# Moving the statistics tile, so that the working buffers begin at a whole kilobyte

## The reference

```python
# first block
proj = rmsnorm(x) @ w_in                       # q_r k_r v_r g_r | q_s k_s v_s | gate_r gate_s
ret = silu(g_r) * retention_chunkwise(q_r, k_r, v_r)      # 4 heads, chunks of 128
swa = swa_gqa_sinks(q_s, k_s, v_s, sinks)                 # 8 heads, window of 128
merged = sigmoid(gate_r) * (ret @ w_ret_out) + sigmoid(gate_s) * (swa @ w_swa_out)
x = x + rmsnorm(merged @ w_out)
x = x + rmsnorm(square(relu(rmsnorm(x) @ w_up)) @ w_down)
# second block
h = x @ w_in_2                                 # pooled part u | q k v | f_logit
mix = concat(pool_mixer(u), forgetting_attention(q, k, v, f_logit)) @ w_out_2
x = layer_norm(ALPHA * x + mix)
x = layer_norm(ALPHA * x + square(relu(x @ w_mlp1_2)) @ w_mlp2_2)
```

## Time and profile before

| | us |
|---|---|
| median of 3 runs | 2570.82 (2569.25 to 2571.11) |
| span of the profiled execution, first to last instruction | 2565.4 |
| TensorE busy | 2522.4 (98%) |
| VectorE busy | 1474.4 (57%) |
| ScalarE busy | 1057.2 (41%) |
| GpSimd busy | 189.9 (7%) |
| transfers, share of 16 engines' span | 38.6% |

### The profile page before, as it was taken

One profiled execution on the slowest core, in us unless ns is written; L12 is line 12 of the kernel. 1 busy time (PEld: TensorE's weight loads), 2 busy tenths in 40 slices (PEclk: granted clock), 3 DMA queues, 4 the chain that ended last, 5 costly groups with the idle time before them and its releaser, 6 DMA issues.

```text
span 2565.4 us, 30682 instructions
## 1 busy us (share of the span) xinstructions
PE 2522.4 (98%) x12072; PEld 2080.6 (81%) x12072; DVE 1474.4 (57%) x2153; ACT 1057.2 (41%) x1698; POOL 189.9 (7%) x173
## 2 busy tenths in 40 slices
PE   7999999999999999999999999999999999999998
PEld 6777888888887788888888887876788888888887
DVE  4345223323533877766764754358768676576668
ACT  4344322223212544444434542357526444444343
POOL 0000000000020200000000110145111000000000
PEclk9999999999999999999999999999999999999999
DMA  4211211111422426547865542101313364488554
GB/s 165 72 69 66 75 41 42 34 33 66 148 83 82 140 89 216 180 156 256 305 256 187 181 158 65 34 20 40 114 51 131 140 223 139 171 324 324 180 193 172
DMA packets 129679, 347.59 MB, mean 135 GB/s; under 512 B 13152, under 2 KB 13408, under 8 KB 129408
## 3 DMA queue, kind: packets, MB, share of 16 engines
q1 hardware_dynamic: 129536, 345.63, 38.6%
HBM read 256.91 MB, written 85.52 MB: 133 GB/s over the span
## 4 chain that ended last, share of the span: by engine, by line
PE 91%; DVE 4%; issue 2%; ACT 1%; DMA 1%; POOL 1%; SPq 0%; DVEq 0%; ACTq 0%; POOLq 0%
PE bank L643 28%; PE bank L645 28%; PE bank L644 28%; DVE PAl L2407 1%; DVE st L2402 1%; PE bank L704 1%; POOL accX L2588 1%; PE bank L754 1%; PE bank L821 1%; PE bank L1070 1%; PE bank L831 0%; PE bank L825 0%; PE bank L789 0%; ACT PAh L1680 0%; DVE wlo L1740 0%
## 5 line engine op out<-in xcount | busy, mean ns | idle before, releaser
L1740 DVE TENSOR_TENSOR wlo<-raw,whi 128x1024 fp32r<-128x1024 f32 x102 | 125.2, 1235 | 253.9 <-ACT whi L1143 253.2
L643 PE MATMUL bank<-hhi,whi 128*128 128x512 f32 x608 | 249.3, 410 | 1.6 <-DVE hlo L1765 1.6
L645 PE MATMUL bank<-hhi,wlo 128*128 128x512 f32 x608 | 238.9, 393 | 0.0
L644 PE MATMUL bank<-hlo,whi 128*128 128x512 f32 x608 | 238.2, 392 | 0.0
L1143 ACT ACTIVATE whi<-raw 128x1024 fp32r<-128x1024 f32 x102 | 106.6, 1054 | 103.8 <-PE bank L645 88.2
L643 PEld LDWEIGHTS bank<-hhi,whi 128*128 128x128 f32 x608 | 114.9, 189 | 29.1 <-issue 6.7
L645 PEld LDWEIGHTS bank<-hhi,wlo 128*128 128x128 f32 x608 | 114.7, 189 | 25.4
L644 PEld LDWEIGHTS bank<-hlo,whi 128*128 128x128 f32 x608 | 115.1, 189 | 22.5
L1448 ACT ACTIVATE r<-r 128x512 f32<-128x512 f32 x78 | 49.1, 629 | 137.6 <-DVE r L2225 100.0
L643 PE MATMUL bank<-yhi,whi 128*128 128x512 f32 x192 | 74.9, 390 | 0.0
L645 PE MATMUL bank<-yhi,wlo 128*128 128x512 f32 x192 | 74.7, 389 | 0.0
(11 more groups left out here) (477 smaller groups left out, 7197.0 us busy)
## 6 DMA issues: line engine op xcount, KB each, us to landing
ra<-ud_d SPq DMA_DIRECT2D x112, 512.0 KB, 4.5
raw<-wp_d SPq DMA_DIRECT2D x102, 512.0 KB, 3.5
rbh<-wp_d SPq DMA_DIRECT2D x64, 512.0 KB, 5.6
rawp<-wp_d SPq DMA_DIRECT2D x26, 1024.0 KB, 5.8
ud_d<-us SPq DMA_DIRECT2D x104, 256.0 KB, 5.4
rbw<-wp_d SPq DMA_DIRECT2D x48, 512.0 KB, 3.6
ud_d<-f SPq DMA_DIRECT2D x76, 256.0 KB, 2.0
rbx<-wp_d SPq DMA_DIRECT2D x32, 512.0 KB, 7.5
```

The lines of the kernel that those rows point to most:

```text
L643: e.matmul(P, sh, mh, start=first, stop=False, skip_group_check=more)
L644: e.matmul(P, sh, ml, start=False, stop=False, skip_group_check=more)
L645: return e.matmul(P, sl, mh, start=False, stop=last, skip_group_check=more)
L1740: e.tensor_tensor(out=wlo[n % SLOTS][:, :], in0=raw[n % RAWS][:, :], in1=whi[n % SLOTS][:, :].bitcast(F32), op=ALU.subtract).then_inc(*up( ...
```

## The change

The region FO begins at 149 KB instead of 149.625 KB behind base, directly behind `maskb`, and `st` moves from in front of the region to behind its last tile. The end of memory in use stays the same. No instruction is added, taken out or moved; the order on all engines is that of before, and only addresses differ.

```diff
-    XO, WO, RO, HO, CO, FO = 0, 32, 72, 84, 148, 149.625
+    XO, WO, RO, HO, CO, FO = 0, 32, 72, 84, 148, 149
...
-    st = at("st", CO + 1, [128, 160])
+    st = at("st", FO + 73.125, [128, 160])
```

## The result

The changed kernel takes 2556.05 us (median of 5 runs, 2555.34 to 2556.62), the kernel before 2570.82 in the same comparison; the ratio is 0.9947, with a 95% interval of 0.9936 to 0.9958. That is 14.8 us less; the interval allows 11 to 16.

A forecast was written before the change was run, and what follows sets the result against it. The prediction took TensorE's matmul spacing as the bound; terms of 1.2, 2.7, 1.0 and 7.9 us made 12.8, less 0.8 gave 12, so span 2553.4 plus 5.4 made 2558.8 us, range 2555.6 to 2562.8.

The forecast's parts named there:

- the phase of two operands: Remainder of a tile's start by 512 bytes; matmuls whose operands differ in it take about 395 ns, not 389.
- the product with mp: Weights mp and mlo in the region, moving whi: 128 matmuls on each of three lines, 2.7 us to gain.
- the fast products: Products of the two MLPs, T1 to T4, h2 and z: 2184 matmuls at 3.6 ns, 7.9 us to gain.
- the two passes of T2 with s24: Weights from the WO buffer took 2.72 us, from the region's 2.79; both forecast to take 2.72.
- the sliding-window output: Moving swahi and swalo in the region, weights whi: 64 matmuls on each of three lines, 1.2 us to gain.
- the product with chi: Last group of the second output product, weights in the region: 192 matmuls at 5 ns, 1.0 us to gain.
- 0.8 us off: Deduction for settling after shape switches and for a possible wait for VectorE from 840 to 890 us.
- the gain is swallowed: Rival: VectorE becomes the bound from 752 to 890 us, leaving 9.1 us, 2561.7; chance counted within the forecast's.
- the 5.4 us: Median of runs above profiled span, 2570.82 against 2565.4, taken as lying around first and last instruction and unchanged.
- the products with hhi: Line 645, 608 matmuls at 393 ns though in one phase: possible extra 2.4 us, in the range's low end.
- No change: Rival: spacing follows distance or what stands next in the stream, not phase, so 2570.8 us; chance 0.13.
- Slower, by transfers: Rival: phase does nothing for TensorE and transfers into the region pay for the lost boundary, 2579 us; chance 0.05.

The follow-up runs named there:

- the kernel before again: The kernel before, unedited, run in the second comparison: 2569.51 us, ratio 1.0002; its profiled execution took 2568.30 us with a span of 2566.5.
- the changed kernel again: The changed kernel, unedited, against the kernel before on one chip: 2555.83 us, ratio 0.9953, span 2553.8.
- the second comparison: Changed kernel, unedited, against the kernel before, on one chip with three of the experiments: 2555.83 against 2568.30 us, ratio 0.9953.

## Why the prediction was right

**The bound and the cause.** That only the spacing of TensorE's matmuls could change, and that it follows the phase of two operands, held at each place shown: swahi and swalo, the product with mp (but for the 393 of its first line), chi and the fast products at 389 to 390, the two passes of T2 with s24 alike, vw0 and rethi unchanged, 20 and 17 more matmuls in the two MLP windows where about 18 in each 270 us were forecast. The experiments make the cause more than an agreement: putting the region 384, 64 or 32 bytes off brings the time of before back, putting it 256 off or moving all together doesn't, and splitting the memory at another place makes other products slow at about the price per matmul that was worked out. What they don't settle is which two reads meet: whether a matmul's own weights count, or the next ones, or both.

**The terms.** From the first matmul of a stage to the first of what follows, the sliding-window output gave 1.26 us (1.2 in the sum). The product with mp gave 1.29 before its last group and 0.26 in it (2.7 together), the product with chi 0.8 (1.0), and the fast products 4.08 and 4.10 (7.9 together). That is 11.8 us, against 12.8 in the sum and 12 in the forecast; the second pair of profiles, of the kernel before again and the changed kernel again, gives 11.8 too. The term that was too large is the product with mp, by 1.1 us: the last group's faster matmuls do little for the beat of its stage, and part of the 8 ns were the five longer rows. The prediction named that place and window, and took 0.8 us off for it together with the settling; the rival "the gain is swallowed" held in this last group, but not before it.

**The step that failed** is the one from the span to the runs. I put the 5.4 us between the profiled span and the median down to what lies around the first and last instruction. Around them lie 1.8 us, in both kernels; the other 3.6 were the spread of executions. It didn't hurt the difference that was forecast, 12 us, which the second comparison shows as 12.5. The first comparison's 14.8 lies beyond the sum and near the low end of the range; nothing in the traces accounts for the surplus. The two first spans differ by 10.6 us, the two of the second comparison, 2566.5 and 2553.8, by 12.7, with 11.8 in the stages named both times; the rest changes from pair to pair, and executions of before spread over 4 us. That 2556.05 fell within the range is in part luck: its low end counts 2.4 us on the products with hhi, which didn't come, and without them the range would have ended at 2558.0. The mechanism and the 12 us don't depend on this.

**The rivals.** *No change*, by two independent reads that never wait: the trace of the changed kernel disagrees, as the earlier trace rows did. What the Trainium skill ("SBUF — State Buffer", Who interferes with whom) says of TensorE's two ports may hold for ports; it doesn't hold as a statement on time, with some 6 ns for each out-of-phase matmul in the run with everything from HO upwards off by 32 bytes. *Slower, by transfers*: the region did lose its 256-byte start, and in the first pair of profiles gs, acc, accX and raw land within 0.2 us of before, those that moved and those that didn't. The extra transaction that the Trainium skill ("DMA: Bandwidth & Descriptors", How a descriptor splits into AXI transactions) counts may be made; the estimate of 0.3 us for a gs isn't seen: 4.5 against 4.4 here, and 4.2 to 4.5 over all profiles with a region off 256 bytes.

## What to carry to other kernels

Where TensorE is the bound, look at the mean of a matmul by line and shape, and compare groups of the same shape: a few ns of difference that follow the tile and not the stage can be a matter of addresses, once the long rows behind waits and transposes are set aside. As far as these runs go (one kernel, one input type, 512 columns), tiles that meet as moving data and weights should begin at the same remainder of 256 bytes; a tile of odd size, like the 640 bytes of statistics here, belongs behind the last of them, not in front. And before a span is set against a median, look at the time of the very execution that was profiled.

## What the runs showed of the hardware

- In a stream of 512-column matmuls of this input type, at a granted clock of 1.00, one starts 227 ns after the other when moving data and weights begin at the same remainder of 256 bytes (43.62 us for the 192 of the sliding-window output), and about 233 when they don't (44.88). The excess isn't confined to the matmul whose operands differ: retlo, in phase, takes 393 ns instead of 389 between neighbours that are out of phase. Which of the two reads gives way, the records don't tell; the weight loads' own records stay at 188 ns.
- In the time of the whole kernel 32 bytes cost what 64 and 128 cost (2569.8, 2568.8 and 2568.6 us), and 256 cost nothing (2556.7). Neither a price that shrinks with the difference nor one that needs 128 bytes fits. Single products differ: with 64 bytes swalo pays nothing (388 ns). Other remainders, 96 and 160 for instance, were not tried for the region alone.
- 256-column matmuls show no price, in the two kinds seen (289 ns out of phase against 290 in phase, and 386 against 385).
